# Second block's mixing stage: convolution by channel halves, softmax work between taps, attention product ahead of the convolution product, branch products in fp32

## The chip, the cores and the metric

The kernel runs on one core of one Trainium2 chip. The metric is the device time of one execution in microseconds (us). The core has five engines that run side by side, each with its own in-order queue, and wait for each other by semaphores: TensorE (PE, matmuls), VectorE (DVE), ScalarE (ACT), GpSimd (POOL) and SyncE (SP, which issues the loads). On-chip memory is SBUF; matmul results land in PSUM.

## The reference, cut to what matters

One sequence of 256 tokens, width 1024, fp32. A first block, then a second block of two layers. The change lies in the mixing stage of those layers (the last line is followed by a gated FFN that isn't touched):

```python
h = rms_norm_2(x, norm1_g[l]) * (1.0 + scale1) + shift1
z = h @ w_in[l]                                  # 1024 x 4608
q, k = partial_rope_2(z[q]), partial_rope_2(z[k])  # 4 heads x 2 x 64
a = softmax(q0 k0) - lam * softmax(q1 k1)        # causal, per head
o = rms_norm_2(a @ v, subln_g[l], eps=1e-5) * (1.0 - lambda_init)
y_attn = o.reshape(b, s, ATTN_W) @ w_attn_o[l]   # 512 x 1024
ga, gb = jnp.split(z[..., C_OFF:G_OFF], 2, axis=-1)
u = ga * jax.nn.sigmoid(gb)
u = causal_depthwise_conv(u, dw_conv_w[l], dw_conv_b[l])   # 31 taps, 512 channels
u = jax.nn.silu(layer_norm(u, conv_ln_g[l], conv_ln_b[l]))
y_conv = u @ w_conv_o[l]                         # 512 x 1024
g_attn, g_conv = jnp.split(jax.nn.sigmoid(z[..., G_OFF:]), 2, axis=-1)
mixed = (g_attn * y_attn + g_conv * y_conv) @ w_out[l]
x = x + (1.0 + gate1) * mixed
```

## The kernel before

Activations lie transposed: channels on the 128 partitions, 256 tokens along the free dimension. Weights come in chunks of 4 x 128 rows by 512 columns (1 MB), in the order of `plan`. A chunk c goes through a ring of three slots: SP loads `raw` once the low part of chunk c-3 is made; ACT makes the rounded high part `hi` (`split`, L728) once PE is through with chunk c-3; DVE makes the low part `lo` = raw - hi (`split`, L1013); PE then does three fp32r products for each tile, hi x hi, hi x lo and lo x hi (`tile_products`, L407), 48 matmuls a chunk. Two PSUM bank pairs alternate between groups of 512 columns (`group_free0/1`). Activations are split the same way into high and low. The two splits run LEAD = 2 chunks ahead: at step c both engines split chunk c+2. Every engine's order is written out by hand.

A layer's mixing, in PE's order: groups 3 and 4 of `w_in` (the two halves of the gated unit `u`), 0 and 1 (queries, keys), 2 (values, token-major), then a loop over eight units i. In each unit PE does one chunk of groups 5 to 8 (the gates), the scores of unit i+1 (a head has two units, one for each softmax), in even units the values product of a head (`apply_v`), in odd units the transposes of the combined probabilities (`turn`) and a head's sum of squares. DVE's unit is: probabilities (L1379 to L1387), `softmax_max(i + 1)`, the copy of a head from PSUM, the low part of chunk i+2, nine taps of the convolution (L1094, 128 channels x 256 tokens each, 124 in all; those before the loop lie between the low parts of the groups 0 to 2, with the rotary steps, L1116 to L1118). ACT's unit is: high part of chunk i+2, exponentials of unit i+1 (L785), then in even units the square of a head, in odd units the transposed probabilities (L789), rstd of a head, the evacuation of a gate group by tanh (L739) and the table load back to exp and log (L746). Behind the taps come the layer norm of the convolution (two sums on PE, L657 and L645) and the products of the conv branch, of the attention branch and of `w_out`; DVE gates and adds the branches (`gate_branch`).

Of the kernel before, what the change touches and what calls it, by code (L numbers as in the profile page):

```python
# [126 lines left out]
def plan(t):  # L127
# [44 lines left out]
def two_blocks(nc, t, consts, out):  # L172
# [38 lines left out]
    for c, (nk, parts) in enumerate(chunks):  # L211
        count[c % RING] += 16 * len(parts)
        landed.append(count[c % RING])

    with ExitStack() as ctx:
# [84 lines left out]
        o_hi = sb("o_hi", [P, GT, S], F32R, on=mixB)  # L300
        o_lo = sb("o_lo", [P, GT, S], F32R, on=mixB)
        uc_hi = sb("uc_hi", [P, GT, S], F32R, on=mixB)
        uc_lo = sb("uc_lo", [P, GT, S], F32R, on=mixB)
# [3 lines left out]
        oB = sb("oB", [P, S], on=mixB)  # L307
# [39 lines left out]

        block = ctx.enter_context(nc.Block())

        @block.sync  # L350
        def _(sp):
# [8 lines left out]
            for c, (nk, parts) in enumerate(chunks):  # L360
# [8 lines left out]
                if c >= RING:  # L369
                    sp.wait_ge(sem("lo_done"), c - RING + 1)  # L370
# [12 lines left out]
        def _(pe):  # L383
# [10 lines left out]
            def full(ins, i):  # L394
                ins.then_inc(sem(f"bank{i}_full"), 1)

# [3 lines left out]
            def tile_products(b0, slot, kk, k, tiles, a_hi, a_lo, ends):  # L400

                w_hi, w_lo = hi[:, slot], lo[:, slot]
                for f in tiles:
                    o = mm[:, b0 + f // 2, (f % 2) * S:(f % 2) * S + S]
                    fs = slice(f * P, f * P + P)
                    for i, (w, a) in enumerate(((w_hi, a_hi), (w_hi, a_lo), (w_lo, a_hi))):
                        ins = pe.matmul(o, w[:, kk, fs], a[:, k, :], start=(k == 0 and i == 0 and f % 2 == 0),  # L407
                                        stop=(ends and i == 2), skip_group_check=True)
                return ins

            def chunk(name, j, a_hi, a_lo, token_major=False, ready=None, per=1):
# [6 lines left out]
                if j == 0 and g >= 2:  # L418
                    pe.wait_ge(sem(f"group_free{g % 2}"), g // 2)
                pe.wait_ge(sem("lo_done"), c + 1)  # L420
                w_hi, w_lo = hi[:, c % RING], lo[:, c % RING]
                b0 = 2 * (g % 2)
                for kk in range(nk):
# [4 lines left out]
                    if token_major:  # L428
                        for tt in range(TT):
                            tok = slice(tt * P, tt * P + P)  # L430
                            for i, (a, w) in enumerate(((a_hi, w_hi), (a_lo, w_hi), (a_hi, w_lo))):
                                ins = pe.matmul(mm[:, b0 + tt, :], a[:, k, tok], w[:, kk, :], start=(k == 0 and i == 0),  # L432
                                                stop=(ends and i == 2), skip_group_check=True)
                    elif not (name in ahead_of_norm and j == len(ids) - 1):
                        ins = tile_products(b0, c % RING, kk, k, range(GT), a_hi, a_lo, ends)
# [1055 lines left out]
```

## Time and profile before

| | us |
|---|---|
| median of 3 runs | 1191.74 (1189.06 to 1193.57) |
| profiled execution, its own time | 1192.61 |
| span of its trace | 1190.8 |
| PE busy | 1126.4 (95%) |
| DVE busy | 844.1 (71%) |
| ACT busy | 547.7 (46%) |
| HBM read | 226.30 MB, 191 GB/s |
| chain that ended last | PE 67%, DVE 23%, ACT 5% |

The busy shares are means over stages with different limits. The trace is best read by stage: layer 0's mixing runs from 396.4 to 584.4 us, layer 1's from 794.4 to 985.1. Matmuls overlap by pipelining, so the distance of two starts tells their cost, not the duration of one. An fp32 matmul shows as two instructions. "Idle before, releaser" tells who ended a wait.

### The profile page before, as it was taken

What the parts mean: (1) busy time and instruction counts of PE and PEld (TensorE: products, weight loads), DVE (VectorE), ACT (ScalarE), POOL (GpSimd) and SP (SyncE); (2) the same over time, 40 slices, a digit from 0 to 9 for tenths busy, and PEclk for the clock granted to TensorE, in tenths of its full rate; (3) what the DMA queues carried; (4) which work ended last, traced back from release to release, by engine and by line L of the source; (5) the groups of instructions that cost most, each with busy time, mean ns of one, the idle gap of its engine ahead of it and who ended that gap; (6) DMA issues with size and microseconds to landing.
All of it is one profiled execution on the core that took longest, in us unless ns stands there. A gap on an engine that the chain in (4) does not pass through costs nothing.

```text
span 1190.8 us, 20043 instructions
## 1 busy us (share of the span) xinstructions
PE 1126.4 (95%) x8620; PEld 1066.4 (90%) x8620; DVE 844.1 (71%) x1131; ACT 547.7 (46%) x605; POOL 12.1 (1%) x26
## 2 busy tenths in 40 slices
PE   5999889999999997989999999999798999999998
PEld 4877688999999896879999999999588899999998
DVE  4955567767664689986688888767989677566452
ACT  3544445565333542575554443354246745444332
POOL 4000000000000000000000000000000000000000
PEclk8999889999999998999999999999989999999998
DMA  6544233787985243434679989946334364766550
GB/s 205 177 133 132 90 125 122 283 302 259 326 299 194 97 152 107 141 107 143 228 247 317 318 291 327 327 136 208 111 107 142 107 206 158 239 221 206 185 167 36
DMA packets 127272, 228.64 MB, mean 192 GB/s; under 512 B 5797, under 2 KB 51219, under 8 KB 127185
## 3 DMA queue, kind: packets, MB, share of 16 engines
q1 hardware_dynamic: 126180, 227.11, 56.5%
q8 instruction: 68, 1.11, 0.4%
q0 software_dynamic: 672, 0.06, 0.1%
q10 hardware_dynamic: 333, 0.21, 0.1%
q14 instruction: 19, 0.16, 0.0%
HBM read 226.30 MB, written 1.05 MB: 191 GB/s over the span
## 4 chain that ended last, share of the span: by engine, by line
PE 67%; DVE 23%; ACT 5%; issue 4%; DMA 1%; SPq 0%; DVEq 0%; ACTq 0%
PE mm L407 58%; DVE cacc L1094 7%; DVE lo L1013 6%; ACT hi L728 3%; PE pv L450 2%; PE pa L464 2%; PE mm L432 1%; DVE ada_acc L1034 1%; DVE hf L1075 1%; DVE qk L1118 1%; DVE hf L1116 1%; DVE qk L1117 1%; DVE hf L1299 1%; PE pv L496 1%; DMA xin<-in_x_dram 1%
## 5 line engine op out<-in xcount | busy, mean ns | idle before, releaser
L1013 DVE TENSOR_TENSOR lo<-raw,hi 128x2048 fp32r<-128x2048 f32 x168 | 380.1, 2266 | 182.7 <-ACT hi L728 179.7
L407 PE MATMUL mm<-act_hi,hi 128*128 128x256 f32 x1760 | 501.0, 285 | 7.1 <-DVE act_lo L1061 5.1
L407 PE MATMUL mm<-act_hi,lo 128*128 128x256 f32 x1760 | 495.3, 281 | 0.0
L407 PE MATMUL mm<-act_lo,hi 128*128 128x256 f32 x1760 | 494.6, 281 | 0.0
L728 ACT ACTIVATE hi<-raw 128x2048 fp32r<-128x2048 f32 x168 | 316.8, 1890 | 203.4 <-PE mm L407 181.2
L407 PEld LDWEIGHTS mm<-act_hi,hi 128*128 128x128 f32 x1760 | 335.0, 190 | 13.5 <-issue 12.2
L407 PEld LDWEIGHTS mm<-act_lo,hi 128*128 128x128 f32 x1760 | 335.0, 190 | 1.0 <-issue 0.7
L407 PEld LDWEIGHTS mm<-act_hi,lo 128*128 128x128 f32 x1760 | 334.5, 190 | 0.0
L407 PE MATMUL mm<-u_hi,hi 128*128 128x256 f32 x608 | 170.6, 281 | 0.0
L407 PE MATMUL mm<-u_hi,lo 128*128 128x256 f32 x608 | 170.4, 280 | 0.0
L407 PE MATMUL mm<-u_lo,hi 128*128 128x256 f32 x608 | 169.2, 278 | 0.0
L407 PEld LDWEIGHTS mm<-u_hi,hi 128*128 128x128 f32 x608 | 114.3, 188 | 0.0
L407 PEld LDWEIGHTS mm<-u_lo,hi 128*128 128x128 f32 x608 | 114.3, 188 | 0.0
L407 PEld LDWEIGHTS mm<-u_hi,lo 128*128 128x128 f32 x608 | 114.2, 188 | 0.0
L1034 DVE SCALAR_TENSOR_TENSOR ada_acc<-ada_raw,ca,ada_acc 128x1024 f32<-128x1024 f32 x84 | 107.6, 1280 | 1.1
L1094 DVE SCALAR_TENSOR_TENSOR cacc<-cu,convw,cacc 128x256 f32<-128x256 f32 x240 | 97.3, 476 | 0.1
L1061 DVE TENSOR_TENSOR u_lo<-sq,u_hi 128x512 fp32r<-128x512 f32 (+1 forms) x30 | 25.0, 834 | 36.2 <-ACT u_hi L898 19.6
L785 ACT ACTIVATE pB<-sB,small 128x128 f32<-128x128 f32 (+1 forms) x32 | 14.3, 446 | 66.7 <-DVEq L1106 66.7
L964 ACT ACTIVATE sq<-mm 128x512 f32<-128x512 f32 x22 | 13.2, 599 | 64.4 <-PE mm L407 64.4
L464 PE MATMUL pa<-sq,cst 128*128 128x256 f32 x128 | 32.5, 398 | 5.3 <-ACT sq L767 5.3
L464 PEld LDWEIGHTS pa<-sq,cst 128*128 128x128 f32 x128 | 23.1, 194 | 13.3 <-ACT sq L767 7.4
L767 ACT ACTIVATE sq<-x 128x512 f32<-128x512 f32 x28 | 17.4, 629 | 33.6 <-DVEq L1333 21.8
(246 smaller groups left out, 1097.3 us busy)
## 6 DMA issues: line engine op xcount, KB each, us to landing
raw<-in_w_in_dram SPq DMA_DIRECT2D x48, 1024.0 KB, 5.1
ada_raw<-in_ada_w_dram SPq DMA_DIRECT2D x96, 512.0 KB, 5.8
raw<-in_w_ffn_in_dram SPq DMA_DIRECT2D x88, 512.0 KB, 5.7
raw<-in_w_ffn_out_dram SPq DMA_DIRECT2D x20, 1024.0 KB, 6.0
raw<-in_w_up_dram SPq DMA_DIRECT2D x16, 1024.0 KB, 6.4
raw<-in_w_down_dram SPq DMA_DIRECT2D x16, 1024.0 KB, 6.8
raw<-in_w_out_dram SPq DMA_DIRECT2D x12, 1024.0 KB, 5.1
raw<-in_w_conv_o_dram SPq DMA_DIRECT2D x4, 1024.0 KB, 5.1
```

What stands on the lines that cost most here:

```text
L407: ins = pe.matmul(o, w[:, kk, fs], a[:, k, :], start=(k == 0 and i == 0 and f % 2 == 0), stop=(ends and i == 2), skip_group_check=True)
L432: ins = pe.matmul(mm[:, b0 + tt, :], a[:, k, tok], w[:, kk, :], start=(k == 0 and i == 0), stop=(ends and i == 2), skip_group_check=True)
L450: ins = pe.matmul(b[:, f:f + 1], ada_acc[:, i % 2, f * P:(f + 1) * P], ones[:, 0:1], start=(f == 0), stop=True, skip_group_check=True)
L464: ins = pe.matmul(pa[:, 0:S], ones, sq[:, k, :], start=(k == 0), stop=(k == KD - 1))
L728: a(act.activation(hi[:, c % RING, 0:nk, :], raw[:, c % RING, 0:nk, :], ACT.Copy), "hi_done")
L767: a(act.activation(sq[:, k, :], x[:, k, :], ACT.Square), "sq_ready")
L785: a(act.activation(p[:, i, lo_:hi_], s[:, i, lo_:hi_], ACT.Exp, scale=-1.0, bias=small[:, 2 + 2 * i + q:3 + 2 * i + q], accum_out=small[:, ...
L964: a(act.activation(sq[:, 0:2, :], complete((l, "ffn", g))[:, 0, :], other(ACT.Silu)), "silu_gate_ready")
L1013: v(dve.tensor_tensor(lo[:, c % RING, 0:nk, :], raw[:, c % RING, 0:nk, :], hi[:, c % RING, 0:nk, :].bitcast(F32), ALU.subtract), "lo_done")
L1034: link(dve.scalar_tensor_tensor(out=acc, in0=w, scalar=ca[:, 1, k:k + 1], in1=acc, op0=ALU.mult, op1=ALU.add), "ada_used")
L1061: ins = dve.tensor_tensor(d_lo, src, h, ALU.subtract)
L1094: v(dve.scalar_tensor_tensor(out=cacc[:, k, :], in0=src, scalar=w, in1=cacc[:, k, :], op0=ALU.mult, op1=ALU.add), name)
```

## The change

- Groups 3 and 4 of `w_in` now each hold 256 columns of both halves of the gated unit, so that after group 3 two of the four channel tiles can be gated and convolved. ACT evacuates each group in two instructions. The 124 taps run half by half, two channel tiles alternating. Their places: `TAPS_AT_IN` behind the chunks of groups 4, 0, 1, 2, `TAPS_IN_UNIT` in the units; the rotary steps stand ahead of a low part.
- DVE's unit is now: `advance` (the low part of chunk i+2), half of the unit's taps, probabilities, the other half, `softmax_max(i + 1)`, in some units a head's norm.
- The scaling of a pair's first probabilities and the reading of a head from PSUM (square and copy, `head_of`) go from DVE to ACT.
- The attention product comes ahead of the convolution product, and its parts are spread head by head between the last steps of attention and of the layer norm (`heads_out`).
- The four chunks of the two branch products are used as fp32 straight from `raw` with unsplit activations: one product for each tile instead of three, no high or low part for them. SP reloads their slots after PE is done with them.

```diff
-TAPS_BEFORE, ROPE_AT, TAPS_AFTER = (13, 13, 9, 12, 7, 12), ("", "", "q", "", "k", ""), (0, 0, 2, 0, 2, 0)
-TAPS_PER_UNIT = 9
-CONV_END = 5
+TAPS_AT_IN = (5, 8, 8, 8, 8, 0, 8, 0)
+TAPS_IN_UNIT = (8, 8, 8, 8, 8, 8, 14, 14)
...
-            group((l, "in", n), w, [(n * GF, GF)], KD)
-        for branch, w_o in (("conv", t["w_conv_o_2"][l]), ("attn", t["w_attn_o_2"][l])):
+            group((l, "in", n), w, [((n + 3) * 256, 256), ((n + 5) * 256, 256)] if n in (3, 4) else [(n * GF, GF)], KD)
+        for branch, w_o in (("attn", t["w_attn_o_2"][l]), ("conv", t["w_conv_o_2"][l])):
...
+    whole = [False] * NCH
+    for name, (_, ids) in groups.items():
+        for c in ids:
+            whole[c] = len(name) == 3 and name[1] in ("attn", "conv")
+    splits = list(np.cumsum([not w for w in whole]))
...
-                    sp.wait_ge(sem("lo_done"), c - RING + 1)
+                    if whole[c - RING]:
+                        sp.wait_ge(sem("mm_done"), c - RING + 1)
+                    else:
+                        sp.wait_ge(sem("lo_done"), int(splits[c - RING]))
...
+                if len(acts) == 1:
+                    return ((raw[:, slot], acts[0]),)
+                a_hi, a_lo = acts
+                return (hi[:, slot], a_hi), (hi[:, slot], a_lo), (lo[:, slot], a_hi)
...
+                if whole[c]:
+                    pe.wait_ge(sem(f"raw_loaded{c % RING}"), landed[c])
+                else:
+                    pe.wait_ge(sem("lo_done"), int(splits[c]))
...
+                heads_out(0, (0, 1))
+                apply_v(ptB, v2, (ATTN_HEADS - 1) * P, P, 0, True)
+                heads_at.append(filled.seen(2))
+                wait("conv_done", GT)
+                mean_of(cacc, 2)
+                heads_out(0, (2,))
+                head_squares()
+                heads_out(1, (0,))
+                wait("csq_ready")
+                mean_of(csq, "a")
+                heads_out(1, (1, 2))
+                heads_out(0, (3,))
+                heads_out(1, (3,))
+                for half in range(2):
+                    chunk((l, "conv", half), 0, csq, ready=None if half else "uc_ready")
...
+                for part in range(2):
+                    name, k = (l, "in", 3 + part), slice(2 * part, 2 * part + 2)
+                    steps(name)
+                    src = complete(name)
+                    a(act.activation(cu[:, k, TAPS - 1:], src[:, 0, :].rearrange("p (a s) -> p a s", a=2), ACT.Copy))
+                    a(act.activation(csq[:, k, :], src[:, 1, :].rearrange("p (a s) -> p a s", a=2), other(ACT.Tanh), scale=0.5), *freed(name))
...
+                def head_of(h):
+                    b = pv[2]
+                    act.wait_ge(sem("bank2_full"), heads_at[l * ATTN_HEADS + h])
+                    a(act.activation(sq[:, 0, :], b[:, 0:S], ACT.Square), "hsq_ready")
+                    if h >= 2:
+                        act.wait_ge(sem("o_ready"), l * ATTN_HEADS + h - 1)
+                    a(act.activation(oB[:, h % 2, :], b[:, 0:S], ACT.Copy), "bank2_free")
+                for i in range(UNITS):
+                    name, j = todoB(l)[i]
+                    split(groups[name][1][j] + LEAD)
+                    if i % 2 == 0:
+                        wait("r_ready")
+                        for q, (lo_, hi_) in enumerate(((0, P), (P, 3 * P))):
+                            a(act.activation(pB[:, 0, lo_:hi_], pB[:, 0, lo_:hi_], ACT.Copy, scale=small[:, 14 + q:15 + q]), "first_scaled")
                     if i + 1 < UNITS:
                         exps(i + 1, sB, pB)
...
                     if i % 2 == 0 and i >= 2:
...
+                        head_of(i // 2 - 1)
+                    if i % 2 == 1:
                         take_turned(ptB[:])
                     if i % 2 == 1 and i >= 3:
...
+                        rstd_from(P, 1, (i - 3) // 2 % 2)
+                    if j == 1:
                         g = name[2] - 5
                         evacuate(name, gates[:, 4 * g:4 * g + 4, :], other(ACT.Tanh), 0.5)
                         log_tables()
...
-                        high(hf[:, h % 2, :], o_hi[:, h, :], "on_ready", "o_hi_ready")
+                head_of(ATTN_HEADS - 1)
+                wait("centred")
+                a(act.activation(csq[:, :, :], cacc[:, :, :], ACT.Square), "csq_ready")
+                rstd_from(P, 1, (ATTN_HEADS - 1) % 2)
+                rstd_from(GF, 1, 0)
+                for k in range(GT):
+                    wait("ln_ready")
+                    a(act.activation(csq[:, k, :], cacc[:, k, :], other(ACT.Silu), bias=pcols(("lnb", l))[:, k:k + 1]), "uc_ready")
...
+                for j, k in [(j, 2 * part + a) for part in range(2) for j in range(TAPS) for a in range(2)]:
...
+                for i, c in enumerate(sum((groups[(l, "in", g)][1] for g in (4, 0, 1, 2)), [])):
+                    if i in (5, 7):
+                        rope(qk2, 1, "q" if i == 5 else "k")
+                    advance(c)
+                    if i == 0:
+                        gated(0)
+                    taps(TAPS_AT_IN[i])
+                    if i == 2:
+                        gated(1)
                 softmax_max(0, sB)
...
+                def probs2(i):
+                    c = i % 2
+                    wait("exp_done", 2)
+                    r = small[:, 14 + 2 * c:16 + 2 * c]
+                    link(dve.reciprocal(r, small[:, 6 + 2 * c:8 + 2 * c]), None if c else "r_ready")
+                    if c:
+                        link(dve.tensor_scalar(r, r, nlam[:, l:l + 1], None, ALU.mult))
+                        wait("first_scaled", 2)
+                        for q, (lo_, hi_) in enumerate(((0, P), (P, 3 * P))):
+                            pc = pB[:, c, lo_:hi_]
+                            v(dve.scalar_tensor_tensor(out=pc, in0=pc, scalar=r[:, q:q + 1], in1=pB[:, 0, lo_:hi_], op0=ALU.mult, op1=ALU.add),
+                              "probs_ready" if q else None)
...
+                def head_normed(h):
+                    v(dve.scalar_tensor_tensor(out=on[:, h, :], in0=oB[:, h % 2, :], scalar=cols[:, 36 + l:37 + l], in1=rstd[:, h % 2, :],
+                                               op0=ALU.mult, op1=ALU.mult), "o_ready")
...
-                for i in range(UNITS + 2):
...
-                            if c == 0:
-                                v(dve.tensor_scalar(pc, pc, r[:, q:q + 1], None, ALU.mult))
...
+                for i in range(UNITS):
+                    name, j = todoB(l)[i]
+                    advance(groups[name][1][j])
+                    count = TAPS_IN_UNIT[i]
+                    taps(count // 2)
+                    probs2(i)
+                    taps(count - count // 2)
                     if i + 1 < UNITS:
                         softmax_max(i + 1, sB)
...
-                        link(dve.tensor_copy(oB[:], full(2)[:, 0:S]), "bank2_free")
...
-                    if i < UNITS - 1:
-                        split(c + LEAD)
-                    if i <= CONV_END:
-                        taps(TAPS_PER_UNIT)
...
-                            low(csq[:, k, :], uc_hi[:, k, :], uc_lo[:, k, :], "uc_hi_ready", "uc_ready")
...
-                        split(c + LEAD)
...
+                    if i % 2 == 0 and i >= 4:
+                        head_normed(i // 2 - 2)
+                taps(GT * TAPS)
+                head_normed(2)
+                n("bank2_full", ATTN_HEADS)
+                v.n("bank2_free", ATTN_HEADS)
+                link(dve.tensor_scalar(hf[:, 2, :], full(2)[:, 0:S], 1.0 / GF, None, ALU.mult), "bank2_free")
+                link(dve.tensor_tensor(cacc[:], cacc[:], hf[:, 2:3, :].to_broadcast([P, GT, S]), ALU.subtract), "centred")
+                head_normed(3)
+                wait("rstd_ready")
+                for k in range(GT):
+                    v(dve.scalar_tensor_tensor(out=cacc[:, k, :], in0=cacc[:, k, :], scalar=pcols(("lng", l))[:, k:k + 1], in1=rstd[:, 0, :],
+                                               op0=ALU.mult, op1=ALU.mult), "ln_ready")
                 for half in range(2):
...
                     gate_branch("attn", half)
...
+                for half in range(2):
+                    steps((l, "conv", half))
+                    gate_branch("conv", half)
+                    for pair in (2 * half, 2 * half + 1):
+                        k = slice(2 * pair, 2 * pair + 2)
                         v(dve.tensor_tensor(gates[:, k, :], gates[:, k, :], gates[:, 8 + k.start:8 + k.stop, :], ALU.add), "mixed_ready")
...
+                    for pair in (2 * half, 2 * half + 1):
+                        k = slice(2 * pair, 2 * pair + 2)
                         low(gates[:, k, :], act_hi[:, k, :], act_lo[:, k, :], "mixed_hi_ready", "mixed_split", scale=0.5)
                 for c in out_chunks(l):
                     advance(c)
```

## Rows read from the trace of the kernel before

**Rows 1.** the page, part 1 and two groups of part 5 (busy us, mean ns | idle before)
```profile
PE 1126.4 (95%) x8620; PEld 1066.4 (90%) x8620; DVE 844.1 (71%) x1131; ACT 547.7 (46%) x605; POOL 12.1 (1%) x26
...
L1094 DVE SCALAR_TENSOR_TENSOR cacc<-cu,convw,cacc 128x256 f32<-128x256 f32 x240 | 97.3, 476 | 0.1
...
L767 ACT ACTIVATE sq<-x 128x512 f32<-128x512 f32 x28 | 17.4, 629 | 33.6 <-DVEq L1333 21.8
```

**Rows 2.** stretches: us, busy PE, PEld, DVE, ACT, POOL, then granted clock, DMA, GB/s
```profile
396.40:584.40 188.00, 173.18 (x1293) 162.46 (x1293) 155.24 (x274) 95.82 (x119) 0.00 (x0) 0.96 0.44 145
...
794.40:985.10 190.70, 175.00 (x1293) 163.98 (x1293) 155.15 (x274) 95.75 (x119) 0.00 (x0) 0.96 0.43 142
```

**Rows 3.** timeline of PE: scores, the chunk behind them, square products later
```profile
463.18 0.79 PE L485 MATMUL pv<-qk 64*128 64x128 f32 x2 [7.04 <-DVE qk L1118]
...
464.75 0.58 PE L407 MATMUL mm<-act_hi,hi 128*128 128x256 f32 x1
...
472.34 0.28 PE L407 MATMUL mm<-act_hi,lo 128*128 128x256 f32 x1
...
588.29 2.75 PE L470 MATMUL pv<-cst 128*128 128x256 f32 x12
```

**Rows 4.** the chain that ended last, 392 to 600 us: start, us, what
```profile
396.45 22.66 PE mm L407 x192
...
424.36 1.29 DVE cacc L1091 x4
...
447.22 2.20 DVE lo L1013
...
462.43 0.70 DVE qk L1118
...
466.24 4.75 DVE cacc L1094 x12
```

**Rows 5.** waits of DVE, 456 to 536 us: total us, times, longest
```profile
DVE lo L1013 <- ACT hi L728: 0.2, 1, 0.2
```

**Rows 6.** the chain, 520 to 536 us
```profile
522.73 1.94 PE pv L657 x8
...
525.15 1.24 DVE cacc L1399
...
529.51 5.61 PE mm L407 x48
```

**Rows 7.** timelines of DVE and ACT, the first unit
```profile
471.46 0.08 DVE L1102 DVE_READ_ACCUMULATOR2_ANT small<- 128x1 f32 x1
...
472.52 1.90 ACT L728 ACTIVATE hi<-raw 128x2048 fp32r<-128x2048 f32 x1
...
474.45 2.29 DVE L1013 TENSOR_TENSOR lo<-raw,hi 128x2048 fp32r<-128x2048 f32 x1 [0.20 <-ACT hi L728]
```

**Rows 8.** timeline of ACT, an odd unit
```profile
497.91 0.40 ACT L785 ACTIVATE pB<-sB,small 128x128 f32<-128x128 f32 x1 [5.26 <-DVEq L1106]
...
502.45 1.28 ACT L746 ACT_TABLE_LOAD   x1
```

**Rows 9.** timeline of DVE, units 1 and 5: start, us, instruction
```profile
480.23 0.16 DVE L1379 RECIPROCAL small<-small 128x2 f32<-128x2 f32 x1
...
480.68 0.75 DVE L1387 SCALAR_TENSOR_TENSOR pB<-pB,small 128x128 f32<-128x128 f32 x2
...
514.31 0.08 DVE L1102 DVE_READ_ACCUMULATOR2_ANT small<- 128x1 f32 x1
```

**Rows 10.** stretches of the loop, columns as in rows 2
```profile
463.20:473.00 9.80, 9.80 (x55) 9.02 (x56) 8.65 (x21) 1.37 (x5) 0.00 (x0) 0.70 0.33 110
...
497.20:505.20 8.00, 8.00 (x60) 7.43 (x61) 7.78 (x21) 6.69 (x12) 0.00 (x0) 1.00 0.39 131
...
879.50:889.20 9.70, 9.66 (x55) 9.22 (x55) 7.12 (x17) 5.46 (x8) 0.00 (x0) 0.69 0.34 109
```

**Rows 11.** DMA issues, 396 to 584 us: KB each, median us to landing
```profile
raw<-in_w_conv_o_dram SPq DMA_DIRECT2D x2, 1024.0 KB, 5.0
```

More of the change, by code:

```diff
@@ L452, in chunk, with product @@
                     full(ins, 2)
[L454 removed]
+            def product(name, *acts, **kw):
                 for j in range(len(groups[name][1])):
[L456 removed]
+                    chunk(name, j, *acts, **kw)
             def sum_squares():
@@ L916, in _ @@
                 exps(0, sB, pB)
-                for i in range(UNITS + 2):
-                    if i < UNITS:
-                        name, j = todoB(l)[i]
-                        split(groups[name][1][j] + LEAD)
-                    else:
-                        split(groups[(l, "conv", i - UNITS)][1][0] + LEAD)
+                def head_of(h):
[5 more added lines that the diff above has]
+                    a(act.activation(oB[:, h % 2, :], b[:, 0:S], ACT.Copy), "bank2_free")
@@ L1352, in taps @@
                         next(conv, None)
-                for c, before, name, after in zip(sum((groups[(l, "in", g)][1] for g in range(3)), []), TAPS_BEFORE, ROPE_AT, TAPS_AFTER):
-                    split(c + LEAD)
-                    taps(before)
-                    if name:
-                        rope(qk2, 1, name)
-                    taps(after)
-                softmax_max(0, sB)
-                def low_of_head(h):
-                    low(hf[:, h % 2, :], o_hi[:, h, :], o_lo[:, h, :], "o_hi_ready", "o_ready")
-                    v.settle()
+                for i, c in enumerate(sum((groups[(l, "in", g)][1] for g in (4, 0, 1, 2)), [])):
[7 more added lines that the diff above has]
+                        gated(1)
+                softmax_max(0, sB)
+                def probs2(i):
[14 more added lines that the diff above has]
+                                               op0=ALU.mult, op1=ALU.mult), "o_ready")
                 def gate_branch(branch, half):
@@ L1418, in _ @@
-                    if i == UNITS - 1:
-                        split(c + LEAD)
-                    if i % 2 == 1 and i >= 3:
-                        h = (i - 3) // 2
-                        wait("rstd_ready")
-                        v(dve.scalar_tensor_tensor(out=hf[:, h % 2, :], in0=oB[:], scalar=cols[:, 36 + l:37 + l], in1=rstd[:, h % 2, :],
-                                                   op0=ALU.mult, op1=ALU.mult), "on_ready")
-                    if i >= UNITS:
-                        gate_branch("conv", i - UNITS)
@@ L1428, in _ @@
+                head_normed(3)
+                wait("rstd_ready")
+                for k in range(GT):
+                    v(dve.scalar_tensor_tensor(out=cacc[:, k, :], in0=cacc[:, k, :], scalar=pcols(("lng", l))[:, k:k + 1], in1=rstd[:, 0, :],
+                                               op0=ALU.mult, op1=ALU.mult), "ln_ready")
                 for half in range(2):
-                    steps((l, "attn", half))
                     gate_branch("attn", half)
-                    pairs = [slice(2 * pair, 2 * pair + 2) for pair in (2 * half, 2 * half + 1)]
@@ L1432, in _ @@
-                    for k in pairs:
+                for half in range(2):
+                    steps((l, "conv", half))
+                    gate_branch("conv", half)
+                    for pair in (2 * half, 2 * half + 1):
+                        k = slice(2 * pair, 2 * pair + 2)
                         v(dve.tensor_tensor(gates[:, k, :], gates[:, k, :], gates[:, 8 + k.start:8 + k.stop, :], ALU.add), "mixed_ready")
-                    for k in pairs:
+                    for pair in (2 * half, 2 * half + 1):
+                        k = slice(2 * pair, 2 * pair + 2)
```

170 lines of the change are left out of this document (56 added, 114 removed).

## Prediction

> **What bounds the kernel now.** I read the totals first, then the stretches by stage, then the waits, the chain and the timelines of the one stage that the change touches. By the totals TensorE (PE) is busy for 1126.4 us [rows 1], but only in the mixing stage of the second block does it leave time unused: in 188.0 us of layer 0 it is busy 173.2, in 190.7 us of layer 1 175.0 [rows 2]. So about 30 us of PE idleness lie where the change is. The largest piece is one wait of 7.04 us for the rotary step of VectorE (DVE) ahead of the first scores [rows 3]. In the chain [rows 4] DVE stands nearly without a gap from 424.36 us on through the unit loop: convolution taps, 2.20 us for each chunk's low part (`split`), softmax pieces. The stage is bound by DVE until the convolution ends, by PE after it. ScalarE (ACT) keeps up because what DVE does next never depends on what ACT has just been given: DVE waited only 0.2 us in all for a high part from 456 to 536 us [rows 5].
>
> **The change, part by part (layer 0, times of the profiled execution).**
>
> *Convolution in halves.* Its first half can start after the first group's product, not the second's. In the run before, DVE works without pause from 424.36 to the last rotary piece's end at 463.13 [rows 4]: 38.8 us for 56 taps, 4 low parts and 2 rotary steps. Afterwards this stretch holds 45 taps, 7 low parts and two gatings: 38.8 + 3 x 2.20 - 11 x 0.396 + 1.3 = 42.3 us; a tap is 4.75/12 = 0.396 us [rows 4]. Two alternating channels instead of four don't slow it: a tap is issued every 0.396 us and lasts 0.476 on the mean [rows 1], shorter than two issues. It starts when the first group ends, 396.45 + 2 x 5.61 = 407.7 [rows 4, 6], plus ACT's half copy 0.6, a table load of 1.28, half tanh 0.6 and a high part 1.8 [rows 1, 7, 8]: about 412.3, hence the rotary ends at 455.1, before PE's last values chunk ends, 7.04 us ahead of 463.18 [rows 3]. Scores start at 456.1 instead. **Gain 7.0 us**, and the slow clock after that wait goes too (below).
>
> *The unit loop, where I expect the loss.* In both kernels ACT's unit i runs: high part of chunk i+2, exponentials of unit i+1, and in odd units the transposed probabilities, rstd, a table load, the gate evacuation, a table load. Before, DVE did `softmax_max(i + 1)` and then split(i+2) and nine taps: ACT's work after that softmax lay beside 2.20 + 3.56 us of DVE work and the next probabilities. Now softmax_max(i+1) is the last step of unit i, and unit i+1 begins with `advance`, the low part of chunk i+3. Its high part stands in ACT's queue behind the exponentials that wait for that very softmax, and in odd units behind the whole tail. Eight taps and the probabilities are queued on DVE behind that wait; PE's transposes and next scores wait for them. The cover is gone and the queues take turns.
>
> Price of a turn: after even units it is what the first unit shows already: softmax ends 471.54, exponentials, high part at 472.52, low part only at 474.45 [rows 7]: 2.9 us; where ACT also squares and copies the head, 0.6 more (each half of the 0.63 for twice the width [rows 1]). After an odd unit, in the run before, exponentials start at 497.91, 0.1 after the softmax, and the second table load ends at 503.73 [rows 8]; a high part of 1.8 follows: 7.7 us in all. The first odd unit has neither rstd (0.9) nor the first table load (1.28): 5.5. So units 0 to 5 wait 2.9 + 2.9 + 5.5 + 3.5 + 7.7 + 3.1 (a head's norm covers 0.4) = 25.6 us. Units 6 and 7 have no low part to make.
>
> DVE's own work in units 0 to 5: six times low part 2.20, 8 taps 3.17, softmax 0.68 = 36.3; reciprocals 3 x 0.19 and combinations 3 x 1.25 [rows 9] = 4.3; a norm 0.4: 41.0 us. The scaling of the first half of a pair and the head copies are now ACT's, 0.7 us each pair and head, inside its time. From the first softmax at 457.3 (455.1 plus a low part): 457.3 + 0.7 + 41.0 + 25.6 = 524.6 for the end of the last of these softmaxes; before, it ended at 514.39 [rows 9]. The probabilities of unit 5 come 0.7 + 1.6 earlier, at 522.3, and from there PE is the bound.
>
> *The tail.* PE from 522.3: two chunks of 5.61 and 3.0 us of small steps (8.0 us of a busy stretch held one chunk and 2.4 of them [rows 10]): 14.2 us, plus 2 us for the slow clock after its 7.7 us of idleness: 538.5. Two heads' products of fp32, 3.4; the last head 0.7; 1.3 waiting for ACT's two reads of it: 543.9. Then without a gap mean, third head, squares, second half's first head, second mean, four more parts, 14.2: 558.1. The norm's chain fits beside it: subtraction 1.24, a narrow step before it, a square of about 1 [rows 6], then rstd, a table load and four silus make the activations ready near 555, 3 us ahead of their use. Conv chunks 4 x 3.44 = 13.8, out chunks 4 x 5.61: 594.3. Before, the same point is 584.0 (the end of the stretch, 584.4, less the step to the squares). **Layer 0: +10.3 us.**
>
> *fp32 products from raw weights*, contained in this: 48 products of split parts take 5.61 us [rows 6], 0.117 each, 0.35 for three. An fp32 product is two instructions; back to back they start every (2.75 - 0.38)/11 = 0.215 us, so 0.43 for one [rows 3]. A chunk of 16 costs 6.9, **+1.27 us a chunk, +5.1 a layer on PE**; by the eight in 1.94 us [rows 6] at most 0.485, +8.6. I take 0.43, since the other figure contains the last one's drain. What it takes away, four high parts and four low parts with the split of the activations, lay mostly beside PE in this tail and buys no more than the sum says.
>
> The Trainium skill, page "FP8 and Floating Point Precision", section "TensorE Precision Notes", says that true fp32 makes four passes through the array. Read against three passes for the three products that would be 4/3 x 0.35 = 0.467 us, an estimate, and 2.4 us more a layer: 1214.4 us. The trace disagrees slightly, with 0.43, and I go by it.
>
> *Queues.* SP now waits for PE to finish a raw chunk before it reloads its slot. The first out chunk's load starts when the last attention product ends, 558.1; landing 5.0 us [rows 11], high and low part 4.2, gating 1.2, mixing 1.2, ACT's high part and the low part 1.3: 571 against its use at 571.9. Cost nothing; with a landing of 6 us it would be 0.3. The groups 3 and 4 come in pieces of 1 KB instead of 2; so do the FFN's chunks, in the stage that follows, where PE is never short of weights; I put nothing on it.
>
> **The sum.** Layer 0: +10.3. Layer 1 is the same schedule, hence as long; but its run before took 190.7 where layer 0 took 188.0 [rows 2], because the clock was low more often: +7.6. Together **+17.9 us**. The profiled execution's own time is 1192.61 (span 1190.8), which gives 1210.5; it lies 0.87 above the median, so against the median I predict **1209.6**.
>
> **The slow clock.** After the 7.04 us wait the granted clock was 0.70 over the next 9.8 us [rows 10], the lower level (1.2 GHz) for part of it: the chunk from 464.75 to 472.62 took 7.87 us instead of 5.87 [rows 3]. That is my 2 us. Inside the new loop such a loss stays hidden: per pair of units PE has 14.3 us of work in 24.7.
>
> **Rivals.**
> (a) *The clock stays low for most of the loop* (slower still). If idleness of 7.7 us in each 24.7 keeps PE at 1.2 GHz, its 42.6 us of work from the first transposes (475.0) to the attention products doubles to 85.2 and PE is the bound: 560.2 instead of 538.5, +21.7 a layer, 1253 us. For it: 0.70 after a single wait, and 0.69 in a stretch of layer 1's loop. Against it: each time 2 us or so of loss and then full speed, as in 497.2 to 505.2 with 1.00 [rows 10]. A part of this, 1 to 16 us in all, is likelier than the whole. The Trainium skill, page "TensorE: Matmul & The Clock Gate", section "HAM oscillation — how this bites in real kernels", describes such a loop, which falls back to the low clock in every pass; no stretch here shows it repeated.
>
> (b) *The turns don't close* (faster). If each high part were ready when DVE comes for it, the 25.6 us a layer would go. PE would then set the time from 456.1 on: eight chunks 44.9 and small steps 12.4, then in the tail 3.4 + 0.7 + 1.5 + 14.2 + 13.8 + 22.4 = 56.0, the end near 569.6: -14.4 and -17.2 in the layers, 1160 us. That needs ACT to have more than 6 us of lead at each `advance`. Against it stands the order of both queues: the exponentials stand ahead of the high part. It decides below 16.6 us of waits a layer: there the kernel is no slower than before.
>
> (c) *The waits are two thirds of mine*, for instance because ACT's steps behind one another cost less than their durations, the rest as summed: no change, about 1192.
>
> (d) *fp32 costs 0.485*: 64 products and 0.055 more each, 3.5 us a layer, 1217.
>
> **Chances.** Forecast with (d) and small parts of (a): 0.72, own range 1201 to 1222. Clock low for long: 0.12, 1222 to 1257. (c): 0.07. (b): 0.09. Two in ten may be left out; so I leave (b), (c) and the far end of (a): 1200 to 1228. About 0.5%, 6 us, is what a measurement of this kernel can tell from no change. Faster by more than it 0.09, within it 0.07, slower 0.84.
>
> **What would show it.** In the profile after, the first scores' wait for the rotary step is gone. DVE's low parts in the loop show waits for ACT's high part, some 25 us a layer against 0.2 before, alternating near 3 and near 8 us; PE's wait for the probabilities is 5 to 8 us, three times a layer. 64 fp32 products a layer at 0.43 us. No wait between the attention, conv and out chunks above 1 us. I am wrong if the low parts don't wait, or if the granted clock in the loop lies under 0.75.

## The result and the profile after

| | before | after |
|---|---|---|
| median, us | 1192.24 (4 runs, 1189.06 to 1193.57) | 1211.33 (4 runs, 1209.03 to 1212.62) |
| profiled execution, us | 1192.61 | 1211.32 |
| span of its trace, us | 1190.8 | 1209.5 |

The ratio is 1.0153, 95% interval 1.0135 to 1.0172: the changed kernel is slower by 1.4% to 1.7%. 1209.6 us had been forecast. The experiments below were measured later, each beside the kernel before, whose median was then 1194.1, 1192.1 or 1191.8 us; so a difference between an experiment and the changed kernel holds to about 2 us.

The stretches by stage come first (columns as in [rows 2]); they answer to those of [rows 2].

```profile
395.50:595.50 200.00, 178.98 (x1228) 165.70 (x1228) 138.93 (x251) 90.39 (x121) 0.00 (x0) 0.95 0.40 135
805.40:1005.40 200.00, 178.66 (x1228) 165.37 (x1228) 138.93 (x251) 90.38 (x121) 0.00 (x0) 0.95 0.40 134
```

A mixing stage now takes 200.0 us in both layers, where it took 188.0 and 190.7. PE is busy 5.8 and 3.7 us longer, DVE and ACT are busy 16 and 5 us less. So 6.2 and 5.6 us more of PE's time is empty although the two other engines have less to do: they wait for each other. The timeline of DVE in the changed kernel's layer 0, the low parts of the first softmax and of units 0 to 5 (in brackets the idle time before, and who ended it), shows where:

```profile
454.65 2.29 DVE L1057 TENSOR_TENSOR lo<-raw,hi 128x2048 fp32r<-128x2048 f32 x1
...
460.42 2.29 DVE L1057 TENSOR_TENSOR lo<-raw,hi 128x2048 fp32r<-128x2048 f32 x1 [2.92 <-ACT hi L768]
...
469.55 2.29 DVE L1057 TENSOR_TENSOR lo<-raw,hi 128x2048 fp32r<-128x2048 f32 x1 [2.91 <-ACT hi L768]
...
482.30 2.29 DVE L1057 TENSOR_TENSOR lo<-raw,hi 128x2048 fp32r<-128x2048 f32 x1 [5.62 <-ACT hi L768]
...
491.82 2.29 DVE L1057 TENSOR_TENSOR lo<-raw,hi 128x2048 fp32r<-128x2048 f32 x1 [3.45 <-ACT hi L768]
...
506.80 2.29 DVE L1057 TENSOR_TENSOR lo<-raw,hi 128x2048 fp32r<-128x2048 f32 x1 [7.86 <-ACT hi L768]
...
516.46 2.29 DVE L1057 TENSOR_TENSOR lo<-raw,hi 128x2048 fp32r<-128x2048 f32 x1 [2.81 <-ACT hi L768]
...
523.51 0.08 DVE L1145 DVE_READ_ACCUMULATOR2_ANT small<- 128x1 f32 x1
```

The six waits of units 0 to 5 add up to 25.6 us; before it was 0.2 [rows 5]. What that does to PE stands in its waits over the stage (us in total, times, longest):

```profile
PE pv L518 <- DVE pB L1422: 18.0, 3, 7.5
PE pv L678 <- ACT oB L967: 1.3, 1, 1.3
PE mm L421 <- DVE act_lo L1101: 1.0, 1, 1.0
```

The wait for the rotary step, 7.04 us in [rows 3], is no longer there. In its place stand three waits for the probabilities, 18.0 us together. The third line was expected to be nothing; the chain of the changed kernel shows what it hangs on:

```profile
550.73 6.92 PE mm L421 x32
557.65 0.02 issue
557.66 7.10 DMA raw<-in_w_out_dram
564.76 0.02 issue
564.78 1.92 ACT hi L768
...
566.79 2.29 DVE lo L1057
569.09 1.14 DVE gates L1435
570.23 0.02 issue
570.25 0.70 DVE gates L1467
...
571.64 0.70 DVE act_lo L1101
```

The load of the first out chunk starts when the last attention product lets its slot go, and takes 7.10 us to land; from there the low part, the gating and the mixing follow in DVE's order.

### The profile page after: what moved, and what is told of

It is laid out like the page before. It is cut to its first block, busy times and chain, and to the rows that moved or that the text cites. A ratio compares the mean times of both kernels' runs of the same rounds, so it can differ in the third digit from the quotient of the medians.

```text
span 1209.5 us, 19727 instructions
## 1 busy us (share of the span) xinstructions
PE 1133.2 (94%) x8492; PEld 1068.1 (88%) x8492; DVE 812.1 (67%) x1085; ACT 536.5 (44%) x609; POOL 12.0 (1%) x26
## 3 DMA queue, kind: packets, MB, share of 16 engines
HBM read 226.30 MB, written 1.05 MB: 188 GB/s over the span
## 4 chain that ended last, share of the span: by engine, by line
PE 73%; DVE 15%; ACT 7%; issue 3%; DMA 2%; SPq 0%; DVEq 0%; ACTq 0%
PE mm L421 63%; DVE lo L1057 5%; ACT hi L768 3%; DVE cacc L1137 3%; PE pv L472 2%; PE pa L486 2%; PE mm L454 1%; DMA raw<-in_w_out_dram 1%; ACT pB L825 1%; ACT L786 1%; DVE hf L1342 1%; DVE sB L1145 1%; DVE hf L1119 1%; PE pv L518 1%; ACT gates L779 0%
## 5 line engine op out<-in xcount | busy, mean ns | idle before, releaser
L1057 DVE TENSOR_TENSOR lo<-raw,hi 128x2048 fp32r<-128x2048 f32 (+1 forms) x160 | 361.9, 2265 | 227.5 <-ACT hi L768 226.3
L768 ACT ACTIVATE hi<-raw 128x2048 fp32r<-128x2048 f32 (+1 forms) x160 | 301.4, 1889 | 217.3 <-PE mm L421 172.9
L518 PE MATMUL pv<-cst,pB 128*128 128x128 f32 x24 | 6.4, 397 | 36.2 <-DVE pB L1422 36.2
L1008 ACT ACTIVATE sq<-mm 128x512 f32<-128x512 f32 x22 | 13.1, 596 | 57.1 <-PE mm L421 57.1
L518 PEld LDWEIGHTS pv<-cst,pB 128*128 128x128 f32 x24 | 3.7, 194 | 38.6 <-DVE pB L1422 38.6
```

The costliest lines, as they stand in the source:

```text
L518: ins = pe.transpose(b[:, i * P:(i + 1) * P], p[:, i * P:(i + 1) * P], ident)
L768: a(act.activation(hi[:, c % RING, 0:nk, :], raw[:, c % RING, 0:nk, :], ACT.Copy), "hi_done")
L1008: a(act.activation(sq[:, 0:2, :], complete((l, "ffn", g))[:, 0, :], other(ACT.Silu)), "silu_gate_ready")
L1057: v(dve.tensor_tensor(lo[:, c % RING, 0:nk, :], raw[:, c % RING, 0:nk, :], hi[:, c % RING, 0:nk, :].bitcast(F32), ALU.subtract), "lo_done")
```

## Experiments

Theory: softmax, exponentials, high part and low part of the two queues take turns, because the low part of a chunk directly follows the softmax on DVE while its high part stands behind that softmax's exponentials on ACT. Rivals: ACT has too much to do with its new work; the fp32 products cost the time; the new distribution of work as a whole, not the place of the low part.

### The low part at the end of the unit

```diff
                 for i in range(UNITS):
                     name, j = todoB(l)[i]
-                    advance(groups[name][1][j])
...
                     if i % 2 == 0 and i >= 4:
                         head_normed(i // 2 - 2)
+                    advance(groups[name][1][j])
```

> The changed kernel with one move: on VectorE `advance` (the low part of chunk i+2) stands at the end of a unit, behind the softmax of unit i+1, not at its start. Theory (turns between the two queues): the high part has then been made while VectorE did taps and probabilities; the low parts' waits for it in the loop, 26 us a layer, fall under 3 us, TensorE is the bound from the first scores on, each layer is 25 us shorter: 1161 us (1157 to 1168). Rival 1 (ScalarE, with the scaling and the head reads that it took over, has too much to do, and the wait only shows at the low part): the waits move to the probabilities, less than 8 us a layer is won, 1195 or more. Rival 2 (the fp32 products are what the time went to): the waits shrink but TensorE stays as late, 1200 or more.

Measured: 1162.62 us, ratio to the kernel before 0.9756 (0.9726 to 0.9786), so 48.7 us less than the changed kernel. Its stretches by stage:

```profile
393.60:568.80 175.20, 172.98 (x1228) 160.10 (x1228) 139.13 (x251) 90.00 (x121) 0.00 (x0) 1.00 0.46 153
779.20:954.80 175.60, 172.67 (x1228) 159.74 (x1228) 139.12 (x251) 89.98 (x121) 0.00 (x0) 1.00 0.45 152
```

24.8 and 24.4 us shorter with the same work on DVE and ACT (139 and 90 us busy in both kernels). In the loop from 453 to 513 us DVE waited for nothing but scores (first line), and PE's waits for the probabilities in the stage fell from 18.0 us to 0.5 (second line):

```profile
DVE sB L1145 <- PE pv L508: 2.5, 2, 1.6
PE pv L518 <- DVE pB L1422: 0.5, 1, 0.5
```

The granted clock is 1.00 instead of 0.95: some 6 us of the 24.8 are PE's busy time, which the slow clock had stretched. ACT's load can't have been the cause, since it is unchanged; nor the fp32 products, which are all there.

### The taps behind the softmax

```diff
                     advance(groups[name][1][j])
                     count = TAPS_IN_UNIT[i]
-                    taps(count // 2)
                     probs2(i)
-                    taps(count - count // 2)
...
                     if i % 2 == 0 and i >= 4:
                         head_normed(i // 2 - 2)
+                    taps(count)
```

> The changed kernel with the taps of a unit behind its softmax instead of around the probabilities; the low part stays first. Theory: eight taps, 3.2 us, now cover part of each turn. Waits of the low parts by unit 0, 0, 2.4, 0.3, 4.6, 0 instead of 2.9, 2.9, 5.6, 3.5, 7.9, 2.8; 12 to 16 us a layer less: 1183 us (1178 to 1189). If the turn is not what sets the loop, the order of taps changes nothing: 1208 to 1214.

Measured: 1182.24 us (ratio 0.9903, 0.9877 to 0.993). DVE's low parts in units 0 to 5 of this kernel:

```profile
462.43 2.29 DVE L1057 TENSOR_TENSOR lo<-raw,hi 128x2048 fp32r<-128x2048 f32 x1 [2.92 <-ACT hi L768]
468.81 2.28 DVE L1057 TENSOR_TENSOR lo<-raw,hi 128x2048 fp32r<-128x2048 f32 x1
478.41 2.29 DVE L1057 TENSOR_TENSOR lo<-raw,hi 128x2048 fp32r<-128x2048 f32 x1 [1.88 <-ACT hi L768]
484.91 2.29 DVE L1057 TENSOR_TENSOR lo<-raw,hi 128x2048 fp32r<-128x2048 f32 x1 [0.20 <-ACT hi L768]
496.74 2.29 DVE L1057 TENSOR_TENSOR lo<-raw,hi 128x2048 fp32r<-128x2048 f32 x1 [4.46 <-ACT hi L768]
503.50 2.29 DVE L1057 TENSOR_TENSOR lo<-raw,hi 128x2048 fp32r<-128x2048 f32 x1
```

Unit 0 keeps its wait, since no taps stand between the first softmax and it (that I had set down as 0 by mistake). Units 1 to 5 wait less by 2.9, 3.7, 3.3, 3.4 and 2.8 us, about the eight taps' 3.2 where the wait was that long. The price of a turn is what ACT does after the softmax less what DVE does in between, and it can be dosed.

### The low part first, in the kernel before

```diff
                 for i in range(UNITS + 2):
                     if i < UNITS:
 
+                        split(groups[todoB(l)[i][0]][1][todoB(l)[i][1]] + LEAD)
                         c = i % 2
...
-                    if i < UNITS - 1:
-                        split(c + LEAD)
                     if i <= CONV_END:
                         taps(TAPS_PER_UNIT)
...
-                    if i == UNITS - 1:
-                        split(c + LEAD)
```

> The kernel before with only the low part of chunk i+2 moved to the start of VectorE's unit, ahead of the probabilities; nine taps stay at its end. Theory: the nine taps (3.6 us) cover the even turns, the odd ones stay open with 2 to 4 us while taps last and with 3 to 5 us in the last units, where there are none: 12 to 14 us a layer: 1219 us (1210 to 1226). Rival (the wait belongs to the new distribution of work, not to the place of the low part): within 3 us of the kernel before, 1189 to 1195.

Measured: 1216.59 us, ratio 1.0199 (1.0176 to 1.0223). The one move makes the kernel before slower than the whole change does. Its waits for high parts in the loop, layer 0, where the kernel before has 0.2 us:

```profile
DVE lo L1013 <- ACT hi L728: 15.0, 5, 4.0
```

They are 2.91, 1.82, 3.98, 3.98 and 2.34 us, and PE's waits for the probabilities grow from 4.5 to 13.1 us. So the place of the low part does it, with the old distribution of work too.

### The scaling back on DVE

```diff
-                    if i % 2 == 0:
-                        wait("r_ready")
...
+                    if not c:
+                        for q, (lo_, hi_) in enumerate(((0, P), (P, 3 * P))):
+                            v(dve.tensor_scalar(pB[:, 0, lo_:hi_], pB[:, 0, lo_:hi_], r[:, q:q + 1], None, ALU.mult), "first_scaled")
```

> The changed kernel with the scaling of a pair's first probabilities back on VectorE; low part first, as in the changed kernel. Theory: the scaling on ScalarE lies beside VectorE's taps and outside the turns, which begin at the softmax's end, so the waits stay within 1 us of the 26 a layer; VectorE has 0.6 us more in three units: 1211 to 1216 us. Rival (ScalarE's new work is what makes the high part late): the waits fall by 2 us a layer or more, 1207 or less.

Measured: 1216.32 us (ratio 1.0204, 1.0187 to 1.0221), 5 us more than the changed kernel. The six waits are 2.92, 2.92, 5.62, 3.44, 7.86 and 2.81 us, the same to 0.01. So the scaling lies outside the turns. The time is just above the expected range; the mixing stages of its trace are 1.2 and 2.0 us longer than those of the changed kernel, about the scaling's 0.6 us in each of three units, and the rest of the 5 us lies outside them.

### Each fp32 product twice

Every product of the two branches is issued a second time, so the branches come out doubled.

```diff
-                    for i, (w, a) in enumerate(pairs):
+                    for i, (w, a) in enumerate(pairs * (2 if len(pairs) == 1 else 1)):
...
-                                        stop=(ends and i == len(pairs) - 1), skip_group_check=True)
+                                        stop=(ends and i == (1 if len(pairs) == 1 else 2)), skip_group_check=True)
```

> The changed kernel with every fp32 product of the attention and conv branches issued twice, so both branches come out doubled: 64 more products a layer on TensorE in a stretch where TensorE is the bound. At 0.43 us each that is 27.5 us a layer, 1266 us (1262 to 1270); at 0.467 us, as four passes of a third of the split product would cost, 1271; at 0.485, 1273.

Measured: 1267.15 us (2 runs, 1265.15 to 1269.15), 55.8 more than the changed kernel for 128 products: 0.436 us each, uncertain by about 0.02 and with some of PE's small waits of the tail gone. The chain is the better measure, since it has 72 products in one piece without a wait:

```profile
559.04 31.08 PE mm L421 x144
```

144 instructions of two a product in 31.08 us are 0.432 us a product. Four passes priced by the split products' (0.467) would be 59.8 us in all and 33.6 in this piece.

### Convolution four channel tiles wide

On top of the kernel with the low part last: groups 3 and 4 as before, the gating behind group 4, taps over four tiles in turn, `TAPS_AT_IN = (0, 0, 10, 12, 11, 0, 12, 0)`.

```diff
-                for j, k in [(j, 2 * part + a) for part in range(2) for j in range(TAPS) for a in range(2)]:
+                for j, k in [(j, k) for j in range(TAPS) for k in range(GT)]:
...
-                    if i == 0:
+                    if i == 2:
                         gated(0)
                     taps(TAPS_AT_IN[i])
-                    if i == 2:
-                        gated(1)
```

> The kernel with the low part last in the unit, and the convolution again four channel tiles wide: groups 3 and 4 hold the two halves of the gated unit as before, the gating waits for group 4, the 45 taps ahead of the loop start some 10 us later. Theory of the sum (the halves buy the earlier first scores): the rotary step ends near 459.5 instead of 455, TensorE waits 4 to 5 us ahead of the first scores and runs slow for a while after it, 4.7 to 6.7 us a layer: 1173 us (1170 to 1177). Rival (with the loop bound by TensorE the early start is worth nothing, the queue of VectorE has room): within 3 us of the kernel with the low part last, 1160 to 1166.

Measured: 1176.76 us (ratio 0.9874, 0.9859 to 0.9889), 14.1 more than with the halves, 7 a layer. PE's first wait is back:

```profile
PE pv L507 <- DVE qk L1159: 3.9, 1, 3.9
```

In the traces the two stages are 5.2 and 7.8 us longer than with the halves. The wait is 3.9 us in both, and the chunk behind it took 7.4 and 8.1 us instead of 5.9, with a granted clock of 0.80 and 0.66 there: 1.5 and 2.3 us. In layer 1 the wait for the mixed low part is also longer, 1.4 us against 0.7. The halves are the part of the change that pays by itself.

### Split branch products

On top of the kernel with the low part last: both branches again with split weights and split activations.

```diff
-            whole[c] = len(name) == 3 and name[1] in ("attn", "conv")
+            whole[c] = False
...
-                        ins = tile_products(2 * (g % 2), ids[0] % RING, k, k, range(GT), (on,), k == GT - 1)
+                        ins = tile_products(2 * (g % 2), ids[0] % RING, k, k, range(GT), (o_hi, o_lo), k == GT - 1)
...
-                    chunk((l, "conv", half), 0, csq, ready=None if half else "uc_ready")
+                    chunk((l, "conv", half), 0, uc_hi, uc_lo, ready=None if half else "uc_ready")
```

> The kernel with the low part last in the unit, and both branch products again of split weights and split activations, three fp32r products a tile (the activations' parts of the convolution branch lie in the FFN's buffers, since SBUF has no room left beside the rest). Theory of the sum (fp32 costs TensorE 0.08 us a product, 64 products a layer, and the removed splits lie beside TensorE): 5.1 us a layer less, 1152 us (1150 to 1156). Rival (what ScalarE and VectorE save by the raw weights is needed in the tail): TensorE waits for the split parts, 1161 or more.

Measured: 1175.44 us (ratio 0.9855, 0.984 to 0.987), 12.8 more, where 10 less was expected. PE's waits in layer 0:

```profile
PE mm L424 <- DVE o_lo L1118: 3.9, 2, 2.2
PE pv L521 <- DVE pB L1435: 3.0, 1, 3.0
PE mm L424 <- DVE gates L1451: 1.1, 1, 1.1
PE pv L681 <- ACT oB L970: 0.8, 1, 0.8
```

Was that the places that I had given the added steps? A second version puts the heads' low parts, the read of the last head and the gating ahead of the weights' low parts, and nine taps in each unit but the last:

```diff
+                    if i == 7:
+                        head_low(1)
                     advance(groups[name][1][j])
-                    if i in (5, 7):
-                        head_low((i - 5) // 2)
+                    if i == 5:
+                        head_low(0)
```

> The kernel of split branch products again, with its steps moved so that none waits for what could come earlier: nine taps in each unit instead of 14 in the last two but one, the heads' low parts ahead of the weights' low parts, the last head read and the gatings ahead of them too. Theory (the first version lost by the places of its steps, and fp32 by itself costs TensorE 5.1 us a layer): the waits, 9 us a layer there, fall under 3, 1152 to 1160 us. Rival (the four chunks' and the activations' low and high parts don't fit beside TensorE's tail wherever they stand, and the raw weights pay for themselves): waits of 5 us a layer or more stay, 1162 us or more.

Measured: 1171.46 us (ratio 0.9821, 0.9785 to 0.9856). The waits:

```profile
PE pv L521 <- DVE pB L1436: 3.4, 1, 3.4
PE mm L424 <- DVE o_lo L1119: 2.5, 1, 2.5
PE mm L424 <- DVE gates L1452: 1.2, 1, 1.2
PE pv L681 <- ACT oB L970: 0.8, 1, 0.8
```

4 us of the 12.8 were the places, 8.8 stay, and the expectation's rival is met: 7.9 us of waits a layer, against 1.8 with raw weights. The largest is mostly DVE's own work: with the attention chunks split, one more weight low part (2.29 us) and a head's (0.42) stand ahead of unit 7's probabilities. The chain passes there through ACT's table load, `ACT hi` 1.93 and `DVE lo` 2.29, but DVE waited for that high part only 0.45 us. The raw weights cost PE 5.1 us a layer by the sum (0.43 us a product instead of 0.35) and, in the two versions built here, earned 9.5 to 11.5 (that cost and half of 8.8 and 12.8). That no order of the split version beats them isn't shown.

### The last head first, then the gating first

Two small moves on the kernel with the low part last. ACT reads the last head ahead of the last gate group's evacuation:

```diff
+                    if i == UNITS - 1:
+                        head_of(ATTN_HEADS - 1)
                     if j == 1:
```

> The kernel with the low part last, and ScalarE reads the last head ahead of the last gate group's evacuation with its two table loads. TensorE's 1.3 us wait for that read goes, in each layer; nothing else is late for it, since the bank of that gate group is needed only 3 us after the evacuation: 1160 us (1158.5 to 1162). If the evacuation is late instead, the wait stands ahead of the second half's first attention product and nothing is won.

Measured: 1162.58 us (ratio 0.9749, 0.9735 to 0.9764), nothing to tell from the kernel without it, where 1160 was expected. PE's wait for the read fell from 1.3 to 0.8 in both layers. In layer 0 another one stands behind it:

```profile
PE pv L678 <- ACT oB L967: 0.8, 1, 0.8
PE mm L421 <- DVE act_lo L1102: 0.8, 1, 0.8
```

It is the load of the first out chunk, whose chain ends last there. The move didn't bring it: the kernel without the move has this wait too, 0.7 us, but in layer 1. In both kernels it stands where that load took longer (6.8 and 6.9 us from issue to landing) and is missing where it took 6.0 and 6.2. So the gating was moved ahead of that chunk's low part:

```diff
                 for half in range(2):
-                    steps((l, "conv", half))
                     gate_branch("conv", half)
...
+                    steps((l, "conv", half))
```

> The kernel with the low part last and the last head read early, with one more move: the conv branch is gated and mixed ahead of the low part of the first out chunk, whose load takes 7.1 us. The chain load, high part, low part, gating, mixing ends ahead of the out chunk only by its first three links, so the wait of TensorE for act_lo (0.8 to 1.0 us a layer) goes; all in all 1.3 to 2.5 us below the kernel with the low part last: 1160.5 us (1158.5 to 1162). If the landing alone sets the out chunk, nothing changes.

Measured: 1161.16 us (4 runs, 1160.69 to 1162.19; ratio 0.9735, 0.971 to 0.9761). The wait for the mixed low part stands in neither layer, PE's waits from the first scores to the end of the layer's mixing come to 1.3 us, and this is the fastest kernel: 2.6% below the one before, 4.1% below the changed one. Against the two before it the gain is inside the intervals, so that the two moves are worth 1.4 us together isn't shown. The load took 6.0 and 6.7 us here; only layer 1, with 6.7, speaks for the second move.

## Why the prediction was right

Taken point by point, for layer 0 (the stage starts 0.93 us earlier in the profile after, at 395.52; times are shifted by that):

| step | forecast | after |
|---|---|---|
| first scores | 456.1 | 456.05 |
| waits of the low parts, units 0 to 5 | 2.9, 2.9, 5.5, 3.5, 7.7, 3.1 = 25.6 | 2.92, 2.91, 5.62, 3.45, 7.86, 2.81 = 25.6 |
| end of the seventh softmax | 524.6 | 524.5 |
| PE takes up unit 5's transposes | 522.3 | 522.4 |
| first mean of the norm | 543.9 | 544.1 |
| conv chunks | 558.1 | 558.6 |
| out chunks | 571.9 | 573.4 |
| end | 594.3 | 596.2 |

The loop was read right in mechanism and in size: the rows of the kernel before already held each turn's price, as the run of ACT's steps from a softmax to a high part [rows 7, 8], and the cover that the change removes could be read from the order of DVE's steps. Moving one line takes the loss away, moving it in the other kernel brings it, covering it in part reduces it in part.

The times met more closely than the working deserves. The rotary's end was put at 455.1, but 412.3 and the 42.3 us of DVE's work make 454.6; it came at 455.5, and the first softmax 0.5 us later than in the sum. DVE's own steps then took 0.5 us less than the 41.7 forecast, and the two cancel in the end of the seventh softmax by luck.

The halves' gain came as summed: 7.0 us of earlier scores. In the kernel with the low part last the halves are worth 7 us a layer, with the slow clock that goes with a wait.

The term of the sum that was mis-sized is the out chunk's load, put at nothing with 0.3 us as its upper price (its own terms give 0.1 for a landing of 6 us). It took 7.10 us to land, not 5.0 [rows 11]: it was issued 1.7 us behind the load of the last conv chunk, when the two attention slots came free one after the other. In the 5 us from its issue on, for 3.3 of which the load ahead was still under way, the 16 DMA engines were busy for 0.96 of the time (columns as in [rows 2]), so the two shared them:

```profile
557.70:562.70 5.00, 5.00 (x25) 4.41 (x24) 1.22 (x1) 0.00 (x0) 0.00 (x0) 1.00 0.96 348
```

PE waited 1.03 us in layer 0 and 1.05 in layer 1 for it. The four out chunks took 22.75 instead of 22.4 us.

These misses make 1.9 us in layer 0 and the same in layer 1 (199.7 us from first product to last, 197.9 forecast). The stages differ by 12.1 and 9.4 us from before, 21.5 together and not 17.9. The forecast time was met more closely than that, because three stretches outside the change came out shorter in this pair of profiles: 0.9 us up to the first layer, 0.3 between the layers, 1.7 after the second. The change doesn't touch them, the runs of the kernel before differ by 4.5 us among themselves, so this part of the agreement is chance.

The slow clock cost less than foreseen, and unevenly. In the three stretches of the profile after that follow a wait of PE for the probabilities, of 5.26, 5.27 and 7.52 us, the chunk took 8.3, 7.3 and 7.0 us instead of 5.9. The fourth line is the whole loop:

```profile
474.60:483.50 8.90, 8.90 (x52) 8.77 (x53) 3.28 (x9) 5.47 (x8) 0.00 (x0) 0.67 0.19 75
498.00:505.60 7.60, 7.60 (x52) 7.38 (x51) 0.95 (x5) 6.47 (x11) 0.00 (x0) 0.80 0.06 25
521.50:529.70 8.20, 8.19 (x54) 7.88 (x54) 7.90 (x23) 5.92 (x11) 0.00 (x0) 0.79 0.22 84
456.00:524.00 68.00, 49.61 (x339) 46.07 (x339) 41.82 (x100) 28.32 (x52) 0.00 (x0) 0.86 0.33 109
```

Only the third is on the path, with 1.1 us where I had put 2. The clock didn't stay low for the loop, with a mean of 0.86, so rival (a) fell. The mean granted clock of the three stretches is 0.67, 0.80 and 0.79, so a part of each ran at the low level, 1.2 GHz, right behind a wait. The page "TensorE: Matmul & The Clock Gate" of the Trainium skill, section "HAM oscillation — how this bites in real kernels", tells of a loop that falls back to the low clock in every pass, and the trace agrees in kind. It cost little because PE had slack in the loop; without the waits the stage's PE work of 179.0 us fell to 173.0.

Rival (b), 1160 us if each high part were ready, was no forecast of this kernel but was met by the one with the low part last, 1162.6: its two layers came out at 24.8 and 24.4 us below those of the changed kernel, where the prediction's two sums lie 24.7 apart (594.3 and 569.6). Rival (d), 0.485 us a product, fell to 0.432 in the doubled products. The page "FP8 and Floating Point Precision", section "TensorE Precision Notes", of the Trainium skill counts four passes; the estimate with a pass priced by the split products' spacing of 0.117 is 0.467. The trace has 0.432, that is 3.7 such spacings, so at least the price of a pass differs; how many passes there are no run here shows.

A sentence of the working was too simple: that what the raw weights take from ACT and DVE "lay mostly beside PE". The sum for the changed kernel holds no term for it, and no run gives the changed kernel its split parts back, so whether it mattered there isn't shown. In the kernel with the low part last it is false: given back, that work brought PE's waits to 8 to 9 us a layer and cost 9 to 13 us in all.

## What to carry to other kernels

When two in-order queues each wait for the other once in a loop, the loop's price is the run of steps on one queue between what it waits for and what it gives, less what the other queue does meanwhile; both can be read from the trace before. So a step that depends on a neighbour's late result belongs at the end of the unit, behind everything that the neighbour needs, and not directly behind the step that sets the neighbour going. Shares of busy time hide this: here DVE and ACT had less to do and the kernel was slower.

Where a slot is freed by the matmul instead of by an early copy, ask when the next loads start, and whether two of them start together.

## What the runs showed of the hardware that was not expected

Two loads of 1 MB issued 1.7 us apart: the second landed 7.10 us after its issue in both layers of the changed kernel, where the median of such loads before was 5.0 [rows 11]. In the layers of four kernels with the low part last and raw branch weights it took 6.0 to 7.5 us, so 7.1 isn't a fixed price.

The length of PE's wait didn't tell what the slow clock then costs: after 5.26, 5.27 and 7.52 us the next chunk lost 2.4, 1.4 and 1.1 us. In the kernel before, waits of 7.04 us (layer 0) and 7.06 us (layer 1) were followed by losses of 2.0 and 1.1 us.
